# A 31-tap depthwise convolution: TensorE takes three taps of the seventh channel tile and seven of the eighth, and its modulation pairs of those tiles go behind the taps

## The reference, cut to what matters

```python
def conformer_conv(h, w_pw1, b_pw1, w_dw, b_dw, ln_g, ln_b, w_pw2, b_pw2):
    u = h @ w_pw1 + b_pw1
    a, g = jnp.split(u, 2, axis=-1)
    v = a * jax.nn.sigmoid(g)
    v = dwconv(v, w_dw, b_dw)            # 31 taps, each channel by itself
    v = jax.nn.silu(layernorm(v, ln_g, ln_b))
    return v @ w_pw2 + b_pw2
```

```python
mod_lat = (sc @ ada_w[i] + ada_b[i])[:, None, :]
mod_ctx = scc @ ada_w[i] + ada_b[i]
```

## Time and the profile before

| | |
|---|---|
| median of 3 runs | 2429.82 us (2429.52 to 2432.27) |
| the profiled execution's own time | 2429.56 us |
| its span in the profile | 2427.7 us |
| busy: PE, DVE, ACT, POOL | 2247.2, 1312.1, 1063.0, 959.2 us |
| mean granted clock of TensorE | 0.96 |
| the convolution's taps on VectorE | from 76.6 to 268.7 us of the span |
| second projection begins | 292.1 us |

### The profile page before, as it was taken

The page is one execution under the profiler, slowest core; times in us unless marked ns, Lnnn a source line. Parts: engine busy times, 40 slices in busy tenths (PEclk is TensorE's granted clock), DMA queues, the critical chain, the costliest instruction groups (busy, mean ns, idle before and its releaser), DMA issues.

```text
span 2427.7 us, 37376 instructions
## 1 busy us (share of the span) xinstructions
PE 2247.2 (93%) x14195; PEld 1876.1 (77%) x14195; DVE 1312.1 (54%) x2205; ACT 1063.0 (44%) x1854; POOL 959.2 (40%) x565
## 2 busy tenths in 40 slices
PE   4999597999999998999989999989987889999998
PEld 3888485899998986767778888867756777778777
DVE  3699828665473745388443223457565536441441
ACT  5666544353352534388444334444453223332431
POOL 1699325464553634200254444433302104444443
PEclk8999897999999998999999999999998989999999
DMA  8788011222222212200123323332200002333332
GB/s 272 253 259 272 20 53 48 61 78 62 65 79 57 83 36 75 70 1 2 52 79 100 108 86 96 104 93 82 80 1 2 2 1 87 91 101 86 90 105 82
DMA packets 338004, 204.81 MB, mean 84 GB/s; under 512 B 6765, under 2 KB 336055, under 8 KB 337847
## 3 DMA queue, kind: packets, MB, share of 16 engines
q1 hardware_dynamic: 332811, 194.03, 26.8%
q10 hardware_dynamic: 5036, 8.66, 1.1%
HBM read 200.47 MB, written 2.19 MB: 83 GB/s over the span
## 4 chain that ended last, share of the span: by engine, by line
PE 56%; issue 20%; DVE 11%; POOL 7%; ACT 3%; DVEq 2%; SPq 1%; DMA 1%; ACTq 0%; POOLq 0%
PE ps L662 12%; PE ps L663 12%; PE ps L664 12%; POOL w_lo L587 6%; DVE ps L1621 5%; PE ps L2151 4%; PE ps L2152 4%; PE ps L2153 4%; PE ps L2456 1%; DVE m L3684 1%; PE ps L3483 1%; PE ps L2484 1%; DMA ada_x<-in_ada_w 1%; PE ps L1713 0%; ACT w_hi L630 0%
## 5 line engine op out<-in xcount | busy, mean ns | idle before, releaser
L587 POOL TENSOR_TENSOR w_lo<-raw,w_hi 128x1024 fp32r<-128x1024 f32 (+3 forms) x199 | 481.5, 2421 | 989.9 <-ACT w_hi L630 973.5
L662 PE MATMUL ps<-x_hi,w_hi 128*128 128x512 f32 (+1 forms) x1256 | 477.3, 380 | 35.4 <-DVE x_lo L1524 13.9
L630 ACT ACTIVATE w_hi<-raw 128x1024 fp32r<-128x1024 f32 (+3 forms) x227 | 241.8, 1065 | 515.5 <-PE ps L664 510.1
L663 PE MATMUL ps<-x_lo,w_hi 128*128 128x512 f32 (+1 forms) x1256 | 463.5, 369 | 0.0
L664 PE MATMUL ps<-x_hi,w_lo 128*128 128x512 f32 (+1 forms) x1256 | 461.9, 368 | 0.0
L662 PEld LDWEIGHTS ps<-x_hi,w_hi 128*128 128x128 f32 x1256 | 244.7, 195 | 90.9 <-issue 24.9
L663 PEld LDWEIGHTS ps<-x_lo,w_hi 128*128 128x128 f32 x1256 | 245.2, 195 | 40.1 <-issue 3.8
L664 PEld LDWEIGHTS ps<-x_hi,w_lo 128*128 128x128 f32 x1256 | 245.0, 195 | 38.1
L662 PE MATMUL ps<-g_hi,w_hi 128*128 128x512 f32 (+1 forms) x704 | 258.7, 368 | 9.2 <-issue 6.8
L663 PE MATMUL ps<-g_lo,w_hi 128*128 128x512 f32 (+1 forms) x704 | 257.2, 365 | 0.0
L664 PE MATMUL ps<-g_hi,w_lo 128*128 128x512 f32 (+1 forms) x704 | 256.7, 365 | 0.0
(11 more groups left out here) (427 smaller groups left out, 4264.0 us busy)
## 6 DMA issues: line engine op xcount, KB each, us to landing
raw<-in_ffn_w_up SPq DMA_DIRECT2D x48, 512.0 KB, 3.8
ada_tail<-in_ada_w SPq DMA_DIRECT2D x22, 1024.0 KB, 7.3
raw<-in_w_up SPq DMA_DIRECT2D x44, 512.0 KB, 3.8
ada_s<-in_ada_w SPq DMA_DIRECT2D x20, 1024.0 KB, 7.8
zq<-in_ffn_w_up SPq DMA_DIRECT2D x80, 256.0 KB, 2.9
raw<-in_conv_w_pw SPq DMA_DIRECT2D x24, 512.0 KB, 6.0
raw<-in_ffn_w_down SPq DMA_DIRECT2D x16, 704.0 KB, 4.5
raw<-in_w_down SPq DMA_DIRECT2D x16, 704.0 KB, 4.6
```

What stands on the lines that cost most here:

```text
L587: pool.tensor_tensor(M.w_lo[:, slot, 0:K * P], M.raw[:, slot, 0:K * P], M.w_hi[:, slot, 0:K * P].bitcast(F32), ALU.subtract).then_inc(lo_r ...
L630: act.activation(M.w_hi[:, slot, 0:K * P], M.raw[:, slot, 0:K * P], ACT.Copy).then_inc(hi_ready, 1)
L662: pe.matmul(o, wh, hi[:, k, t0:t0 + tn], start=first, stop=False)
L663: pe.matmul(o, wh, lo[:, k, t0:t0 + tn], start=False, stop=False)
```

## The change

TensorE does 3 taps of tile 6 and 7 taps of tile 7, where it did 1. VectorE's share falls from 20 taps to 18 and 14; ScalarE and GpSimd keep 10, with other tap numbers. The added diagonal matrices (2 and 6) are made by ScalarE (`diag_act`), at the end of its work on the tile ahead. `gated(7)` comes after 9 of VectorE's taps of tile 6 instead of 12. On TensorE the pairs 16 and 17 move from ahead of chunk 15 to behind the taps of tile 7, and pair 18 too; `turn_mods_pe` moves behind `mean_pe`. On VectorE `ada_rest_dve` moves behind `mean_dve`. On ScalarE the last five tap products of tile 7 move ahead of `copy_conv(6)`. ScalarE's wait for `mod_ready` after `pw1_act` stays as it is. SyncE's list is not edited.

```diff
-PE_TAPS = 1
+PE_TAPS = (1, 1, 1, 1, 1, 1, 3, 7)
...
-        self.diag = [[diag[i][:, n, :] for n in range(PE_TAPS)] for i in (0, 1)]
+        diag += [at(f"diag{i + 2}", r_wlo + i * w + behind_8, [3, P]) for i in (0, 1)]
+        self.diag = [[diag[0][:, n, :] for n in range(3)], [diag[i][:, n, :] for i in (1, 2, 3) for n in range(3)]]
...
         pe.wait_ge(v_ready, done(j + 1))
         pe.wait_ge(diag_ready, done(j + 1))
-        for tap in range(PE_TAPS):
+        for tap in range(PE_TAPS[j]):
+            if tap == 1:
+                pe.wait_ge(diag_more, sum(PE_TAPS[:j + 1]) - j - 1)
             for t0, t1, at in ((0, SEQ, VLAT), (SEQ, TOK, VCTX)):
...
         for j in range(1, 8):
             first, *others = pairs_of(j)
-            chunk(2 * j + 1)
-            ada(first)
             if j < 7:
+                chunk(2 * j + 1)
+                ada(first)
                 chunk(2 * j + 2)
-            taps_pe(pe, j)
-            for n in others:
-                ada(n)
-        turn_mods_pe(pe)
+                taps_pe(pe, j)
+                for n in others[:2 if j < 6 else 0]:
+                    ada(n)
+            else:
+                chunk(2 * j + 1)
+                taps_pe(pe, j)
+                for n in (*pairs_of(6)[1:], first, *others):
+                    ada(n)
...
-    DVE_TAPS = TAPS - PE_TAPS - POOL_TAPS
-    NEXT_AT = 12
+    DVE_TAPS = [TAPS - n - POOL_TAPS for n in PE_TAPS]
+    NEXT_AT = (12, 12, 12, 12, 12, 12, 9)
...
+            if j == 7:
+                for n in range(5, POOL_TAPS):
+                    tap_act(act, j, n)
             if j:
                 copy_conv(act, j - 1)
             groups_to(pairs_of(j)[1])
-            for n in range(5, POOL_TAPS):
+            for n in range(5, POOL_TAPS) if j < 7 else ():
                 if j < 6 and n == POOL_TAPS - 1:
                     weights(2 * j + 5)
                 tap_act(act, j, n)
+            if j in (5, 6):
+                diag_act(act, j + 1)
...
     def mean_pe(pe):
 
         pair = Q0["pw2"] % 4
-        pe.wait_ge(evac, done(Q0["pw2"] - 4))
+        pe.wait_ge(evac, done(Q0["pw2"] - 2))
...
-        for tap in range(PE_TAPS):
+        c = COL["conv_w_dw"] + j
+        pool.tensor_scalar(M.diag[j % 2][0], ident, M.prm[:, c:c + 1], None, ALU.mult).then_inc(diag_ready, 1)
+
+    def diag_act(act, j):
+
+        for tap in range(1, PE_TAPS[j]):
             c = COL["conv_w_dw"] + tap * 8 + j
-            ins = pool.tensor_scalar(M.diag[j % 2][tap], ident, M.prm[:, c:c + 1], None, ALU.mult)
-        ins.then_inc(diag_ready, 1)
+            act.activation(M.diag[j % 2][tap], ident, ACT.Identity, scale=M.prm[:, c:c + 1], bias=0.0).then_inc(diag_more, 1)
...
             if st == "ln":
                 mean_pe(pe)
+                turn_mods_pe(pe)
                 ln_pe(pe)
...
             if st == "ln":
                 mean_dve(dve)
+                ada_rest_dve(dve)
...
                 pw1_dve(dve)
-                ada_rest_dve(dve)
```

More of the change, by code:

```diff
@@ L464, in build_in @@
     diag_ready = sem("diag_ready")
+    diag_more = sem("diag_more", False)
     pe_taps = sem("pe_taps")
@@ L1002, in taps_pe @@
                                M.vp[:, j % 3, at - PAD + tap:at - PAD + tap + t1 - t0], start=(tap == 0),
-                               stop=(tap == PE_TAPS - 1))
+                               stop=(tap == PE_TAPS[j] - 1))
         mm.then_inc(pe_taps, 1)
@@ L1585, in build_in, with steps_before @@
     VLAT, VCTX = PAD, SEQ + 3 * PAD
-    DVE_TAPS = TAPS - PE_TAPS - POOL_TAPS
-    NEXT_AT = 12
+    DVE_TAPS = [TAPS - n - POOL_TAPS for n in PE_TAPS]
+    NEXT_AT = (12, 12, 12, 12, 12, 12, 9)
+    def steps_before(j):
+        return sum(2 * n + 1 for n in DVE_TAPS[:j])
     def pw1_dve(dve):
@@ L1607, in pw1_dve @@
             dve.wait_ge(pe_taps, done(j + 1))
-            for i in range(DVE_TAPS):
-                if i == NEXT_AT and j < 7:
+            for i in range(DVE_TAPS[j]):
+                if j < 7 and i == NEXT_AT[j]:
                     gated(j + 1)
-                tap = PE_TAPS + POOL_TAPS + i
+                tap = PE_TAPS[j] + POOL_TAPS + i
                 for n, (t0, t1, at) in enumerate(((0, SEQ, VLAT), (SEQ, TOK, VCTX))):
@@ L1617, in pw1_dve @@
                     o = M.pair(j % 2, t0, t1)
-                    step = (2 * DVE_TAPS + 1) * j + 2 * i + n
+                    step = steps_before(j) + 2 * i + n
                     if i:
@@ L1622, in pw1_dve @@
                         .then_inc(tap_done, 1)
-            dve.wait_ge(tap_done, done((2 * DVE_TAPS + 1) * (j + 1) - 1))
+            dve.wait_ge(tap_done, done(steps_before(j + 1) - 1))
             dve.wait_ge(pool_tap, done(SUMS * (j + 1)))
@@ L1634, in tap_act @@
             if j >= 2:
-                act.wait_ge(tap_done, done((2 * DVE_TAPS + 1) * (j - 1)))
+                act.wait_ge(tap_done, done(steps_before(j - 1)))
         elif m >= PT_RING:
@@ L1638, in tap_act @@
         dst = M.pt[:, m % PT_RING, :] if n else M.pc[:, j % 2, :]
-        tap = PE_TAPS + n
+        tap = PE_TAPS[j] + n
         c = COL["conv_w_dw"] + tap * 8 + j
@@ L1700, in copy_conv @@
         pair = j % 2
-        act.wait_ge(tap_done, done((2 * DVE_TAPS + 1) * (j + 1)))
+        act.wait_ge(tap_done, done(steps_before(j + 1)))
         act.activation(M.cv[:, j, :], M.pair(pair), ACT.Identity, bias=M.col("conv_b_dw", j)).then_inc(cv_ready, 1)
```

## The result

The changed kernel takes 2450.14 us in the median of 4 runs (2446.46 to 2451.53), the kernel before 2431.05 us in 4 runs (2429.52 to 2432.97). The ratio is 1.0075, interval 1.0062 to 1.0088: 18.2 us slower (15.1 to 21.4, of 2431). Forecast were 2442.2 us, range 2437.0 to 2446.6. The direction held, the time lies above the range. The profiled execution (2446.46 us, span 2444.5) is the shortest of the four; its span is 16.8 us longer than that of before.

The account below looks back on a forecast made before the run. VectorE was taken to bound the last convolution tile, then TensorE's chain through the mean. Late pairs 3.8, ScalarE's wait 7.3 and clock 1.5 gave 12.6 us on 2429.56: 2442.2 us, range 2437.0 to 2446.6.

Parts of the forecast that it names:

- Parts 1 to 3: Taps of tiles 6 and 7, gated(7), matrices and sums riding along free: VectorE's list gains 6.8 us, ending at 262.8.
- Part 4: Weight pairs behind TensorE's last taps: pair 19 starts only at 263.1, so the mean ends 3.8 us later, at 276.1.
- Part 5: ScalarE's unmoved wait for mod_ready holds the squares until ada_rest_dve, now behind the mean's subtraction: 7.3 us more.
- Part 6: Sums of squares (ln_pe) on TensorE start at 1.2 GHz after about 9 us idle: 1.5 us more, between 0 and 3.
- The sum: Delay before the second projection: 3.8 + 7.3 + 1.5 = 12.6 us, giving 2442.2 us from 2429.56.
- so the shift goes on whole: Stages behind: the second projection waits for the first normalized tile, so all 12.6 us reach the whole time.
- No change: Rival: VectorE's gain reaches the mean, which ends 7.1 us early; +1.7 us, 2431.3 us; chance 0.03.
- ScalarE is not held: Rival: mod_ready's count is reached earlier, so only the pairs' +3.8 us stays, 2433.4 us; chance 0.04.
- Faster: Rival: later matmul runs shift against the clock's changes and give back 17.5 us or more; chance 0.02.

Follow-up runs that it names:

- r1: The changed kernel again, unedited, beside the kernel before: 2444.68 us in 6 runs, ratio 1.0062.
- e2: The changed kernel with pairs 16, 17 and 18 back where they were in TensorE's list: 2434.14 us, ratio 1.0016.
- e6: The changed kernel with one tap on TensorE for every tile and gated(7) behind 12 taps, all moves kept: 2439.93 us, ratio 1.0034.
- e7: The changed kernel with unused small products filling TensorE's idle time ahead of pairs 18, 19 and the sums of squares: 2439.99 us, ratio 1.0040.
- e1: The changed kernel with ScalarE's wait for mod_ready moved from behind pw1_act to just ahead of pw2_act: 2436.22 us, ratio 1.0031.
- r2: The kernel before again, unedited, for a second profile of it: ratio 1.0009.
- e4: The kernel before with only a delay of 13 scratch multiplications on VectorE ahead of the mean's subtraction: 2445.13 us, ratio 1.0062.
- e3: The changed kernel with ScalarE's wait moved ahead of pw2_act and pairs 16, 17 and 18 put back: 2427.08 us, ratio 0.9988.
- e9: As e8, with unused small products ahead of the mean, its last tile and the sums of squares: 2421.54 us, ratio 0.9972.
- e8: The changed kernel with ScalarE's wait moved, pair 16 ahead of chunk 15, pair 17 between chunk 15 and the last tile's taps: 2424.99 us, ratio 0.9988.

## Why the prediction was right and wrong

**Parts 1 to 3 (taps, `gated(7)`, what rides along): right.** VectorE waited 1.61 us ahead of the seventh tile (forecast 1.55), `gated(7)` came at 235.64 (235.65), the taps at 236.83 (236.85), the last tile at 247.14 (247.05), the last add ended at 262.9 (262.8). The six diagonal matrices took 1.84 us on ScalarE. Only the clock ahead of the taps was left open: it held here and fell in r1, where the taps took 1.65 us longer and VectorE waited 0.67 (forecast up to 1.5, and 0.5).

**Part 4 (the pairs): the mechanism right, the size short by 1.8 us.** That the pairs' move delays the mean is shown by e2, and with one tap on TensorE (e6) the same move did not delay it. The mean ended at 277.88, 5.6 us late, where I had 3.8. From the issue of pair 18 to the first product of pair 19 it took 15.93 us, not 15.04; the pair ran wholly at half clock (3.31 against my middle of 2.65); the mean took 10.53 against 10.4. The same four loads took between 14.5 us (e6) and 17.4 us (e7) from that issue to that product, so one measured 15.04 could not carry the term to a microsecond. The estimate from the Trainium skill's fit (DMA: Bandwidth & Descriptors, Anatomy of one DMA) was 11.6 us and missed by 4.3: its figure is for one transfer on GpSimd's path, and these loads were issued by SyncE. No run here shows what sets the pace of these loads.

**Part 5 (ScalarE's wait): right.** 8.30 - 1.07 = 7.2 us (forecast 7.3), shown by e1 and seen again in e2 and e6. The Trainium skill (TensorE: Matmul & The Clock Gate, Architectural detail) calls ScalarE's queue a strict first-in first-out: e1 agrees, in that moving one wait down the list let the squares begin 1.05 us behind the mean and not 8.30.

**Part 6 (clock at the sums): right, 1.74 us for 1.5.** Shown by e1 and e7.

**The sum.** 5.6 + 7.2 + 1.7 = 14.5 us in the stage, where I had 12.6; from 2429.56 that is 2444.1, inside the range. **What failed is the step "so the shift goes on whole", as it was used for the range:** I gave the stages behind no spread, and took the base from one execution. From the forecast to the measured median it is 7.9 us. Of these 1.9 lie in the stage, nearly all of it Part 4's term. Another 2.3 lie behind it in the profiled execution: from the reciprocal to the end of the span it took 2144.5 us, before 2142.3. The last 3.7 are the distance of the four executions' median from the profiled one; the kernel before has 1.5 of such a distance (2431.05 against 2429.56), which my base left out.

The stretch behind the reciprocal took 2145.5 us in r2, with no edit at all, and 2144.6 in r1. So the profile's 2.3 us are less than what two profiles of the kernel before differ by, 3.2. The times go together with the granted clock: in r2's twelve executions the shortest has 2421.40 us at 0.963 and the longest 2435.65 at 0.955; the changed kernel's four have 0.955 (2446.46 and 2449.73 us) and 0.953 (the two others). I had put chance in the clock of the later stages only into a rival of 0.02 that needed 17.5 us at once, and not into the range, though the kernel before spreads from 2421.3 to 2435.1 in 29 runs. With 3 us more at either end the range would have been 2434.0 to 2449.6, still just short of 2450.14; the second comparison's 2444.68 lies inside even the range as it stood.

That the surplus over the stage is chance is supported by r1's and e4's medians and by r2, not proved. One thing speaks against it: the profiles of the changed kernel and of r1 wander alike, 3 us down between 1300 and 1645 and 6 up between 1900 and 2000, where pure chance was expected to differ; e1 and e3 share the first of these steps, e4, e7 and r2 don't. What decides each step stays open.

**The rivals.** "No change" and "ScalarE is not held" are refuted by the chain. "Faster" by chance didn't happen. The gain of the exchange is real, 6.8 us on VectorE's list; it was spent on an idle wait. Most of it reaches the time once the two orders are mended: 5.9 us of the stage in e9.

## What to carry to other kernels

When a piece of work is moved on one engine, look at every fixed wait of the other engines on its count, not only at those beside the move: here one wait, untouched and free before, cost 7.2 us. When uses of a buffer ring are moved back, move the issue of its next loads back in mind too, and price the last load from its own issue, with the spread that the same loads show elsewhere. And a shift of a few microseconds in a program of 2.4 ms should be read from the stage in the profile; for the whole time the range must carry what two runs of the same program differ by.

## What the runs showed of the hardware

The granted clock is not a fixed function of the gap: after the same 2.4 us of idle time the seven taps ran at full clock in one run (9.30 us) and partly at 1.2 GHz in another (10.95), and after 1.94 us the sums of squares took 10.64 us in e1 and e8 and 12.31 in e3. Small products in the gaps went with a clock of 1.00 in every such place of the one profile of e7 and the one of e9.
